# Two-layer hybrid decoder step: where SyncE requests the retention states' stores, and where the retention mixer's engines meet

## The reference

```python
def _layer(x, past, prm):
    h = _rmsnorm(x, g)
    p = _split_cols(jnp.einsum('nld,dc->nlc', h, w_in))
    ret_o, ret_s = _retention(p['ret_q'], p['ret_k'], p['ret_v'], q_pos, ret_s0)
    ...
    mix = jnp.concatenate([ret_o * silu(p['ret_g']), ...], axis=-1)
    x = x + jnp.einsum('nlc,cd->nld', mix, w_out)

def _retention(q, k, v, pos, s0):
    def step(S, inp):
        ...
        S = S * s_dec[None, :, None, None] + jnp.einsum('nkhd,nkhe->nhde', kc * k_dec[None, :, :, None], vc)
        return S, o
    S, o = lax.scan(step, s0, (_blocks(q, chunk), _blocks(k, chunk), _blocks(v, chunk)))
    o = o * lax.rsqrt(jnp.mean(o * o, axis=-1, keepdims=True) + NORM_EPS)
    return o, S
```

## Time and profile before

| | us |
|---|---|
| median of 3 runs (lowest, highest) | 2986.56 (2983.92, 2989.94) |
| the profiled execution's own time | 2984.37 |
| its span, first to last instruction | 2982.6 |
| PE busy (share of the span) | 2766.2 (93%) |
| DVE busy | 1489.8 (50%) |
| ACT busy | 916.9 (31%) |
| mean granted TensorE clock, as a share of 2.4 GHz | 0.962 |

### The profile page before, as it was taken

One profiled execution on the slowest core, in us unless ns is written; L12 is line 12 of the kernel. 1 busy time (PEld: TensorE's weight loads), 2 busy tenths in 40 slices (PEclk: granted clock), 3 DMA queues, 4 the chain that ended last, 5 costly groups with the idle time before them and its releaser, 6 DMA issues. The chain is left out here.

```text
span 2982.6 us, 61447 instructions
## 1 busy us (share of the span) xinstructions
PE 2766.2 (93%) x25518; PEld 2550.5 (86%) x25518; DVE 1489.8 (50%) x2602; ACT 916.9 (31%) x1742; POOL 147.8 (5%) x301
## 2 busy tenths in 40 slices
PE   6998999999899997989989989999988999887998
PEld 6997988897787987889989889889977788887997
DVE  4332253336745585963343323532477267589433
ACT  3222253223222342232232223432322225422322
POOL 2100000000011000000002000000000200000001
PEclk8999999999999899989999999999999989998999
DMA  5322334732233222034333233265322422300543
GB/s 184 91 69 73 82 106 114 205 106 72 51 93 84 57 65 88 3 106 137 109 81 92 54 91 98 79 192 156 92 54 56 110 57 66 106 19 5 160 134 132
DMA packets 398476, 278.01 MB, mean 93 GB/s; under 512 B 34460, under 2 KB 368332, under 8 KB 394606
## 3 DMA queue, kind: packets, MB, share of 16 engines
q1 hardware_dynamic: 397278, 263.50, 31.9%
q10 hardware_dynamic: 912, 10.50, 0.9%
HBM read 237.75 MB, written 36.18 MB: 92 GB/s over the span
## 5 line engine op out<-in xcount | busy, mean ns | idle before, releaser
L326 PE MATMUL acc<-h_hi,in_w_hi 128*128 128x272 f32 x3968 | 896.3, 307 | 28.7 <-SPq L511 16.9
L326 PE MATMUL acc<-h_hi,in_w_lo 128*128 128x272 f32 x3968 | 830.1, 291 | 0.0
L326 PE MATMUL acc<-h_lo,in_w_hi 128*128 128x272 f32 x3968 | 829.4, 291 | 0.0
L326 PEld LDWEIGHTS acc<-h_hi,in_w_hi 128*128 128x128 f32 x3968 | 636.7, 192 | 114.3 <-issue 68.3
L326 PEld LDWEIGHTS acc<-h_lo,in_w_hi 128*128 128x128 f32 x3968 | 633.9, 192 | 0.0
L326 PEld LDWEIGHTS acc<-h_hi,in_w_lo 128*128 128x128 f32 x3968 | 630.6, 192 | 0.0
L356 DVE TENSOR_TENSOR in_w_lo<-in_w_raw,in_w_hi 128x512 fp32r<-128x512 f32 x496 | 349.2, 710 | 418.0 <-ACT in_w_hi L352 415.1
L352 ACT CAST in_w_hi<-in_w_raw 128x512 fp32r<-128x512 f32 x496 | 303.2, 617 | 393.0 <-PE acc L326 303.0
L326 PE MATMUL dr_bank<-over_both,out_weights 128*128 128x272 f32 x1984 | 280.2, 288 | 1.7 <-DVE over_both L716 1.7
L326 PEld LDWEIGHTS dr_bank<-over_both,out_weights 128*128 128x128 f32 x1984 | 260.8, 188 | 2.0 <-DVE over_both L716 2.0
L356 DVE TENSOR_TENSOR out_weights<-regions,out_weights 128x512 fp32r<-128x512 f32 x128 | 88.2, 691 | 183.5 <-ACT out_weights L352 183.3
(11 more groups left out here) (417 smaller groups left out, 3317.9 us busy)
## 6 DMA issues: line engine op xcount, KB each, us to landing
in_w_raw<-in_w_in SPq DMA_DIRECT2D x488, 256.0 KB, 2.9
region<-in_cache_sb_kv SPq DMA_DIRECT2D x128, 256.0 KB, 3.1
regions<-in_w_out SPq DMA_DIRECT2D x128, 256.0 KB, 2.8
regions<-in_cache_dsa SPq DMA_DIRECT2D x64, 160.0 KB, 2.2
region<-x_spill SPq DMA_DIRECT2D x32, 272.0 KB, 3.4
x_spill<-region SPq DMA_DIRECT2D x32, 272.0 KB, 2.1
mix_spill<-mix SPq DMA_DIRECT2D x6, 1088.0 KB, 5.5
mix_back<-mix_spill SPq DMA_DIRECT2D x6, 1088.0 KB, 7.4
```

The costliest lines, as they stand in the source:

```text
L326: last = pe.matmul(self.place(i)[:, c, 0:HALF_N], w[:, u % RING, t, :], part[f][:, HALF_N * c:HALF_N * c + HALF_N], start=first and w is k ...
```

## The change

SP's generator no longer goes straight to the end of the mixer. It waits 24 marks, requests the stores of `p_ret`, waits five more, requests those of `s_ret`, and goes to the end, where `store.wait()` and the meeting stand. The last `yield` in front of the meeting is repeated five times in PE's, ACT's and DVE's generators: PE gives 15 steps there in place of 3, and so twelve of the steps that came behind the meeting come ahead of it. POOL's generator isn't touched. No instruction is added or taken away.

```diff
     def pe(self, pe):
...
             last.then_inc(self.summed, 1)
             yield 3
-        yield 3
+        for _ in range(5):
+            yield 3
         meet(pe, self.left, 1)
...
     def act(self, act):
...
-        yield
+        for _ in range(5):
+            yield
         meet(act, self.left, 1)
...
     def dve(self, dve):
...
-        yield
+        for _ in range(5):
+            yield
         meet(dve, self.left, 1)
...
     def sp(self, sp):
...
-        yield LAST
+        yield 24
         sp.wait_ge(self.carried, QB)
         for h in range(4):
             r, j = h % 2, h // 2
             store(k.p_ret[bass.ds(l, 1), 0, h].rearrange("a d e -> (a d) e"), self.state[64 * r:64 * r + 64, j, r, :])
+        yield 5
         sp.wait_ge(self.advanced, 4)
         for h in range(4):
             store(k.s_ret[bass.ds(l, 1), :, h].rearrange("a s d e -> (a d) s e"), self.state_s[64 * (h % 2):64 * (h % 2) + 64, :, h // 2, :])
+        yield LAST
         store.wait()
         meet(sp, self.left, 1)
```

## The result

| | before | after |
|---|---|---|
| median, us (lowest to highest) | 2985.24 (2980.6 to 2989.94) | 2963.62 (2961.82 to 2967.04) |
| profiled execution's own time, us | 2984.37 | 2961.82 |
| its span, us | 2982.6 | 2959.9 |
| mean granted TensorE clock | 0.962 | 0.967 |

A forecast was written before the change was run, and what follows sets the result against it. The prediction took PE, busy 93% of the span, to bound the kernel. Idle time of 16.2 us plus slow stretches of 4.9 us made 21.1 us less than the median of 2986.56: 2965 us, range 2960 to 2975.

The forecast's parts named there:

- What PE waited for: At retention's meeting PE waits 16.9 us in two waits for SP's drain, late by requesting and landing stores.
- Term 1: PE's idle time at the meeting in both layers goes, except 0.37 us each: 16.2 us less.
- Term 2: The half-clock stretch of PE behind the meeting goes in both layers: 4.9 us less, bounds 0 to 4.9.
- The requests ahead of weight loads: On SP's queue, one weight load comes 1.0 us late behind s_ret: cost 0, bound 1.2 us a layer.
- The stores' bytes: Store bytes meeting weight bytes on DMA cost 0; the skill's ring order would make the sum about 2 us smaller.
- The twelve steps: PE reaches the new meeting 8.9 us later, leaving the stores 8.6 us of margin to land.
- The rival "slower": Stores queued on SP starve PE's weight stream behind them; at 25 us late the kernel takes 2996 us; chance 0.02.
- L - 12.3 + 2.4: Price in us a layer when the next weights come L late: lateness less cover, plus 2.4 for slow clock.
- cover of 12.3 us: Weight lateness hidden from PE, worked out from old states' loads that held SP 13.5 us and cost 1.2.

The follow-up runs named there:

- the two filled holes: Kernel before, with 36 or 18 matmuls on constants put between PE's drain and its wait at the meeting: 2990.10 us and 2985.12 us.
- the kernel with the far meeting: Changed kernel with s_ret stored by 32 requests in place of four and the meeting sixty steps further down: 2984.05 us.
- the later stores: Changed kernel with the s_ret stores requested five marks later, six steps ahead of the meeting: 2968.94 us.

## Why the prediction was right, point by point

- **What PE waited for.** Right: the two waits for SP's drain are gone and nothing took their place. The stores alone give the whole gain, the steps alone none, and `p_ret`'s requests alone 3.0 us of each hole.
- **Term 1**, 16.2 us. Right, 0.6 us too small: PE idles 0.09 us at the new meetings, not the 0.37 taken from the earlier trace rows, which makes it 16.8. At the later mixers' meetings PE waits for another engine's drain; here it is the last to come. SP's drain started at 270.9 and PE's ended at 272.6, so SP was 1.6 us ahead, as worked out (1.7). DVE was 2.3 us ahead, where I gave it 0.7, because I had put its drain behind its last part of a piece. The rows of the kernel after show the two side by side, and together they end at 270.3:

```profile
269.62 0.69 DVE L356 TENSOR_TENSOR in_w_lo<-in_w_raw,in_w_hi 128x512 fp32r<-128x512 f32 x1 [2.08 <-ACT in_w_hi L352]
...
L511 DVEq DRAIN  x1: 730/730/730, 269.6 to 269.6; - x1
```

- **Term 2**, 4.9 us. Right in size (10.9 + 10.6 us of stretch, less 16.8, leaves 4.7), and its cause is shown by the two filled holes, not only argued: the clock behind them stayed at 1.00. The time of a launch did not show it.
- **The requests ahead of weight loads**, 0. Right: no wait for `in_w_lo` was added. The load behind `s_ret` stood at 260.07; it was 1.3 us late, not 1.0. But the price of a late load had been misread from the earlier trace rows. Around PE's longest wait there the kernel before has

```profile
126.58 0.62 ACT L352 CAST in_w_hi<-in_w_raw 128x512 fp32r<-128x512 f32 x1 [4.90 <-DMA in_w_raw<-in_w_in]
...
140.26 1.79 DVE L1258 TENSOR_TENSOR region<-region,regions 128x544 f32<-128x544 f32 x1 [0.72 <-POOL region L1326]
141.97 0.72 DVE L356 TENSOR_TENSOR in_w_lo<-in_w_raw,in_w_hi 128x512 fp32r<-128x512 f32 x1
142.75 0.52 PE L326 MATMUL acc<-h_hi,in_w_hi 128*128 128x272 f32 x2 [0.98 <-DVE in_w_lo L356]
```

The piece that PE waited for had been rounded by 138.6; DVE came to it late because of the mixer's own work, the last of it at L1258. ACT's wait of 7.13 us at 145.70 was for a load which SP requested at 142.86, as soon as DVE's part had freed its buffer. What follows the sixteen loads is ACT's wait of 4.90 us, and it cost PE nothing that the rows show.
- **The stores' bytes**, 0. Right for PE, but the earlier trace rows could not show it: the weight load of that row did not run beside the stores. It was requested when their bytes had just gone by (kernel before; the DMA share is the last but one number):

```profile
382.00:383.00 1.00, 1.00 (x7) 0.78 (x6) 0.82 (x2) 0.15 (x1) 0.00 (x0) 1.00 1.04 356
383.00:384.00 1.00, 1.00 (x10) 1.00 (x9) 0.96 (x3) 0.60 (x2) 0.00 (x0) 1.00 0.15 41
383.03 0.42 SPq L343 DMA_DIRECT2D in_w_raw<-in_w_in  x1
```

Beside the stores of `s_ret` weight loads landed in 3.0 to 4.1 us (255 to 266 us of the kernel after), not in 2.9. The longest is the load right behind the stores, 1.3 us over the usual 2.8. The Trainium skill ("DMA: Bandwidth & Descriptors", "Queues, rings and completion order") has descriptors consumed in ring order, and the trace agrees with it in sign; the 3.4 us that I had worked out from it were too much. ACT waited for no load there.
- **The twelve steps.** The prediction's 8.6 us of margin for the stores came from the 8.9 us of the twelve steps: by its own times the stores would have landed 0.3 us too late without them. Without them SP's drain in fact started 0.7 us before PE's pipe was empty. So the steps were not needed in these runs.
- **The rival "slower".** Its price formula, L - 12.3 + 2.4 a layer, gives 10.0 at L = 19.9; measured, the kernel with the far meeting is 20.4 us above the changed one's 2963.62, 10.2 a layer. That its cover of 12.3 us came so near the 11.7 measured is luck, because it was worked out from the misread rows; that L is 19.9 in both is chance too, since in the rival it came from four landings in a row and here from 32 requests. And its place was wrong for this kernel: with a meeting twelve steps behind the stores, SP's lateness reaches PE at the meeting first, 11.66 us, before the weights run out.

## What to carry to other kernels

A store that must have landed before a barrier should be requested so early that requests and landing end ahead of the slowest engine's arrival; how early is read from three rows: the requests' duration, the landing, and the time at which the bounding engine reaches the barrier. The queue that it moves into may be held for as long as its buffers cover, but if the same sequencer also has to come to the barrier, it is its own lateness there that counts first. A hole of the bounding engine costs more than its length where the clock falls behind it: look at the granted clock in the stretch behind the hole.

## What the runs showed of the hardware that was not expected

The length of a hole of PE did not settle whether the clock fell behind it. With the later stores the clock fell behind 2.10 us in layer 1 and stayed at 1.00 behind 2.28 us in layer 2. At the wait for the cache it stayed at 1.00 behind 1.27 us (kernel before) and 1.70 us (the twelve steps alone), and fell behind 1.85 and 2.13 us (18 matmuls in the hole). Later in layer 1, behind a hole of 2.6 us at one and the same line of the program, it was 0.50 in the kernel before (at 1009.6 us) and 1.00 in the one after (at 998.8 us). Behind every hole of 5.4 us and more at retention's meeting it fell. So a gain of clock at one place can be lost at another.

Splitting a store doesn't split its requests' time: four requests of 256 KB held SP for 3.5 us, 32 requests of 32 KB for the same bytes 21.7 us, 0.68 us each. A drain's record need not stand behind the engine's last operation: DVE's lay beside it.
